# Stick-breaking values with the value block stationary: two heads on 64 output partitions each, split from the bank without transposes

## What is computed

```
h = rmsnorm(x, norm_mix_g);  proj = h @ w_in          # q, k, v of all branches are column ranges of proj
z = einsum('bhqd,bshd->bhqs', q * d**-0.5, k)
log_beta = log_sigmoid(z)
log_1m = where(key < query, log_beta - z, 0)
cum = cumsum(log_1m over keys)
a = where(key < query, exp(log_beta + cum[-1] - cum), 0)
y_sb = einsum('bhqs,bshd->bqhd', a, v)                # [256, 16 * 64]
merged = sig(g_ml)*(y_ml @ w_ml_proj) + sig(g_sc)*(y_sc @ w_sc_proj) + sig(g_sb)*(y_sb @ w_sb_proj)
x = x + merged @ w_out;  x = x + relu(rmsnorm(x) @ w_up)**2 @ w_down;  then the second block
```

## Time and profile before

| | |
|---|---|
| three runs | 957.66, 960.19, 960.67 us; median 960.19 |
| the profiled execution | 958.35 us, of which 956.4 us from first to last instruction; 1.95 us around it |
| TensorE busy | 927.4 us, 97% of the span |
| VectorE, ScalarE, GpSimd busy | 578.9, 469.4, 38.6 us |
| granted TensorE clock, mean | 0.991 of full |
| stick-breaking, from the first scores to the last values | 92.7 to 216.1 us |
| transposes of its result | from 272.8 us |

### The profile page before, as it was taken

One profiled execution on the slowest core, in us unless ns is written; L12 is line 12 of the kernel. 1 busy time (PEld: TensorE's weight loads), 2 busy tenths in 40 slices (PEclk: granted clock), 3 DMA queues, 4 the chain that ended last, 5 costly groups with the idle time before them and its releaser, 6 DMA issues.

```text
span 956.4 us, 14152 instructions
## 1 busy us (share of the span) xinstructions
PE 927.4 (97%) x6003; PEld 841.2 (88%) x6003; DVE 578.9 (61%) x610; ACT 469.4 (49%) x520; POOL 38.6 (4%) x75
## 2 busy tenths in 40 slices
PE   5999999999999999999999999998999799999996
PEld 5998998899998888888999988897888699999885
DVE  4555646577787445556556654556886666666552
ACT  6344776862445434344555534445744554444341
POOL 0000111120010000000000000010000000000000
PEclk9999999999999999999999999998999899999999
DMA  7577444443255556555555565537612465555641
GB/s 266 193 250 229 137 168 139 133 148 117 89 176 177 198 198 195 201 177 198 176 177 177 176 220 181 194 91 247 215 52 87 155 197 178 176 177 198 203 149 44
DMA packets 99374, 164.01 MB, mean 171 GB/s; under 512 B 4832, under 2 KB 37315, under 8 KB 99184
## 3 DMA queue, kind: packets, MB, share of 16 engines
q1 hardware_dynamic: 99312, 163.11, 52.0%
HBM read 162.03 MB, written 3.16 MB: 173 GB/s over the span
## 4 chain that ended last, share of the span: by engine, by line
PE 93%; DVE 2%; DMA 2%; ACT 2%; issue 1%; SPq 1%; POOL 0%; DVEq 0%; ACTq 0%; POOLq 0%
PE acc L509 14%; PE acc L513 14%; PE acc L511 14%; PE acc L501 14%; PE acc L503 14%; PE acc L502 14%; DMA land<-in_w_in 2%; PE m L528 1%; PE m L575 1%; PE m L564 1%; PE m L553 1%; DVE wlo L1211 0%; ACT lw L989 0%; DVE x_tok L1487 0%; PE m L609 0%
## 5 line engine op out<-in xcount | busy, mean ns | idle before, releaser
L1211 DVE TENSOR_TENSOR wlo<-land,whi 128x2048 fp32r<-128x2048 f32 (+2 forms) x153 | 337.1, 2207 | 237.8 <-ACT whi L866 235.2
L866 ACT ACTIVATE whi<-land 128x2048 fp32r<-128x2048 f32 (+2 forms) x153 | 282.3, 1849 | 229.0 <-PE acc L503 156.7
L509 PE MATMUL acc<-xT_hi,whi 128*128 128x256 f32 x1168 | 335.2, 287 | 2.1 <-DVE xT_lo L1248 1.8
L513 PE MATMUL acc<-xT_hi,wlo 128*128 128x256 f32 x1168 | 332.2, 284 | 0.0
L511 PE MATMUL acc<-xT_lo,whi 128*128 128x256 f32 x1168 | 332.1, 284 | 0.0
L509 PEld LDWEIGHTS acc<-xT_hi,whi 128*128 128x128 f32 x1168 | 225.8, 193 | 7.1 <-issue 5.4
L511 PEld LDWEIGHTS acc<-xT_lo,whi 128*128 128x128 f32 x1168 | 225.9, 193 | 0.1
L513 PEld LDWEIGHTS acc<-xT_hi,wlo 128*128 128x128 f32 x1168 | 225.8, 193 | 0.0
L501 PE MATMUL acc<-whi,xT_hi 128*128 128x512 f32 (+2 forms) x240 | 91.4, 381 | 0.0
L503 PE MATMUL acc<-whi,xT_lo 128*128 128x512 f32 (+2 forms) x240 | 90.2, 376 | 0.0
L502 PE MATMUL acc<-wlo,xT_hi 128*128 128x512 f32 (+2 forms) x240 | 90.1, 375 | 0.0
(11 more groups left out here) (337 smaller groups left out, 1074.5 us busy)
## 6 DMA issues: line engine op xcount, KB each, us to landing
land<-in_w_in SPq DMA_DIRECT2D x56, 1024.0 KB, 5.1
land<-in_w_up SPq DMA_DIRECT2D x16, 1024.0 KB, 5.3
land<-in_w_down SPq DMA_DIRECT2D x16, 1024.0 KB, 5.1
land<-in_w_ffn_gate SPq DMA_DIRECT2D x22, 512.0 KB, 4.0
land<-in_w_ffn_up SPq DMA_DIRECT2D x22, 512.0 KB, 5.2
land<-in_w_ffn_down SPq DMA_DIRECT2D x10, 1024.0 KB, 5.1
land<-in_w_out SPq DMA_DIRECT2D x6, 1024.0 KB, 5.0
land<-in_w_in SPq DMA_DIRECT2D x12, 512.0 KB, 4.5
```

Of the source, the lines that this page charges most:

```text
L509: mm(to, whi[:, s, k, cs], xh[:, k0 + k, :], start=first and c % 2 == 0, stop=False, skip_group_check=True)
L513: last = mm(to, wlo[:, s, k, cs], xh[:, k0 + k, :], start=False, stop=end, skip_group_check=True)
L866: activate(whi[:, u % PARTS, 0:m, 0:w], land[:, u % LANDS, 0:m, 0:w], ACT.Copy).then_inc(hi_ready, 1)
L1211: v.tensor_tensor(wlo[:, u % PARTS, 0:m, 0:w], land[:, u % LANDS, 0:m, 0:w], whi[:, u % PARTS, 0:m, 0:w].bitcast(F32), ALU.subtract).then_ ...
```

## The change

The roles in `sb_values` are swapped: the 64 columns of `sbv` that belong to a head are the stationary operand (128 rows by 64 columns), the weights `sba` the moving one. A head's result then has its 64 features on partitions: head h on partitions 0 to 63 and head h+1 on 64 to 127 of the same bank `M[h % 4]`, 256 queries in its first 256 columns. That is the layout the projection takes: tile h // 2 of `ysbT`. `sb_result` becomes a ScalarE copy of 128x256 to `ysbT_hi` and a VectorE subtraction to `ysbT_lo`, once a pair. The stage "ysb" of transposes, with its copies and subtractions, goes. `sb_scores` takes both heads of a pair in one call, the two 256-column matmuls ahead of the two 128-column ones. `sb_av` and `sb_y` count pairs. In the diff the first new `sb_result` is ScalarE's, the second VectorE's.

```
-TURNS = [("x", KD, "norm_mix_g"), ("ysb", KD, None), ("yml", KD, "ml_norm_g"), ("merged", KD, None),
+TURNS = [("x", KD, "norm_mix_g"), ("yml", KD, "ml_norm_g"), ("merged", KD, None),
...
             elif act == "ysbT":
-                turned_ready("ysb", k1)
+                pe.wait_ge(sb_y, k1)
...
         def sb_scores(h):
             if h >= 4:
-                pe.wait_ge(sb_y, h - 3)
+                pe.wait_ge(sb_y, h // 2 - 1)
...
-            c, o = h // 2, SB_D * (h % 2)
-            z = M[h % 4]
-            mm(z[:, 0:T], sbkT[o:o + SB_D, c, 0:P], sbqT[o:o + SB_D, c, :], start=True, stop=True)
-            mm(z[:, T:T + P], sbkT[o:o + SB_D, c, P:T], sbqT[o:o + SB_D, c, P:T], start=False, stop=True,
-               skip_group_check=True).then_inc(sb_z, 1)
+            c = h // 2
+            for i in range(2):
+                hs = slice(SB_D * i, SB_D * (i + 1))
+                mm(M[(h + i) % 4][:, 0:T], sbkT[hs, c, 0:P], sbqT[hs, c, :], start=True, stop=True)
+            for i in range(2):
+                hs = slice(SB_D * i, SB_D * (i + 1))
+                mm(M[(h + i) % 4][:, T:T + P], sbkT[hs, c, P:T], sbqT[hs, c, P:T], start=False, stop=True,
+                   skip_group_check=True).then_inc(sb_z, 1)
...
         def sb_values(h):
-            pe.wait_ge(sb_am, h + 1)
-
-            o, a = M[h % 4][:, 3 * P:], sba[:, h % 2]
-            v = slice(h * SB_D, (h + 1) * SB_D)
-            for to, parts in ((o[:, 0:SB_D], ((0, 0),)), (o[:, SB_D:], ((P, 0), (T, 1)))):
-                for at, t in parts:
-                    last = mm(to, a[:, at:at + P], sbv[:, t, v], start=False, stop=True, skip_group_check=True)
+
+            pe.wait_ge(sb_am, h + 2)
+            to = M[h % 4]
+            for i in range(2):
+                mm(to[SB_D * i:SB_D * (i + 1), 0:T], sbv[:, 0, (h + i) * SB_D:(h + i + 1) * SB_D],
+                   sba[:, i, 0:T], start=True, stop=False, skip_group_check=True)
+            for i in range(2):
+                last = mm(to[SB_D * i:SB_D * (i + 1), P:T], sbv[:, 1, (h + i) * SB_D:(h + i + 1) * SB_D],
+                          sba[:, i, T:3 * P], start=False, stop=True, skip_group_check=True)
             last.then_inc(sb_av, 1)
...
-            if u == TURN_SB:
-                pe.wait_ge(sb_y, SB_H)
-                pe.wait_ge(ml_y, ML_H)
-                turn("ysb", tok)
...
+        def sb_result(h):
+            act.wait_ge(sb_av, h // 2 + 1)
+            activate(ysbT_hi[:, h // 2, :], M[h % 4][:, 0:T], ACT.Copy).then_inc(sb_y_hi, 1)
...
+            if u - SB0 in range(4, SB_H + 3, 2):
+                sb_result(u - SB0 - 4)
             moba_weights((u - 1, UNITS[u - 1][2]))
             if u != LAST_U["mix1"]:
                 split(u + 2)
...
         def sb_result(h):
-            dve.wait_ge(sb_av, h + 1)
-            v.tensor_copy(tok[:, :, h * SB_D:(h + 1) * SB_D],
-                          M[h % 4][:, 3 * P:].rearrange("p (t d) -> p t d", t=TT)).then_inc(sb_y, 1)
+            dve.wait_ge(sb_y_hi, h // 2 + 1)
+            v.tensor_tensor(ysbT_lo[:, h // 2, :], M[h % 4][:, 0:T], ysbT_hi[:, h // 2, :].bitcast(F32),
+                            ALU.subtract).then_inc(sb_y, 1)
```

More of the change, by code:

```diff
@@ L337, in build @@
         sem(n) for n in ("sb_z", "sb_log", "sb_t", "sb_tm", "sb_r", "sb_a", "sb_am", "sb_av", "sb_y"))
-    sig_o = sem("sig_o")
+    sb_y_hi = sem("sb_y_hi")
     ml_s, ml_w, ml_wm, ml_p, ml_num, ml_y, ml_ss, ml_rs, yml_ready = (
@@ L602, in ml_scores @@
                 pe.wait_ge(sb_a, SB_H)
-                pe.wait_ge(sb_y, SB_H)
+                pe.wait_ge(sb_y, SB_H // 2)
                 pe.wait_ge(read_dve, reads_before(G_AT["mlv1"], "dve"))
@@ L819, in _ @@
                     sb_scores(i)
-                    sb_scores(i + 1)
             if i % 2 == 1 and 3 <= i <= SB_H + 1:
                 sb_values(i - 3)
-                sb_values(i - 2)
             i = u - ML0
@@ L920, in sb_weights @@
             if h >= 2:
-                act.wait_ge(sb_av, h - 1)
+                act.wait_ge(sb_av, h // 2)
             activate(sba[:, h % 2], M[h % 4][:, 0:3 * P], ACT.Exp).then_inc(sb_a, 1)
+        def sb_result(h):
+            act.wait_ge(sb_av, h // 2 + 1)
+            activate(ysbT_hi[:, h // 2, :], M[h % 4][:, 0:T], ACT.Copy).then_inc(sb_y_hi, 1)
         def ml_weights(h):
@@ L1121, in _ @@
                 activate(gate[:], acc[:, n % 2], ACT.Sigmoid).then_inc(read_act, 1)
-            if u == TURN_SB:
-                turn_split("ysb", ysbT_hi)
             if u == TURN_ML:
@@ L1530, in _ @@
                 sb_result(u - SB0 - 4)
-                sb_result(u - SB0 - 3)
             if u == B2 + 2:
@@ L1634, in _ @@
             if u == TURN_SB:
-                turn_split("ysb", ysbT_hi, ysbT_lo)
                 dve.wait_ge(ml_rs, 1)
```

## The result

The change takes the median from 960.43 us (four executions, 957.66 to 961.77) to 952.93 us (four, 952.22 to 954.0): a ratio of 0.9919, with a 95% interval of 0.9898 to 0.9940. That is 7.5 us by the medians and 7.8 by the ratio, where the forecast was 4.55 us, or 0.47%. The sign was right and the size was not: the gain is 1.6 to 1.7 times the forecast. The ratio applied to the 960.19 us of the prediction gives 952.4, just under its range; the measured median itself lies just inside.

A forecast was written before the change was run, and what follows sets the result against it. TensorE, busy 97%, was taken as the bound. Transposes 1.75 plus eight values blocks 2.8 made 4.55 us off: 953.8 from the profiled 958.35, 955.6 from the median; forecast 955.0 us, range 952.7 to 957.8.

The forecast's parts named there:

- the clock: Rival: behind TensorE's long second-block waits, a 1.2 GHz stretch comes or goes, about 3 us either way; chance 0.04.
- The sum: TensorE's work: 1.75 us for removed transposes plus 2.8 us for eight values blocks, 4.55 us saved, bounds 4.05 and 4.75.
- The transposes: Near 272.82 us on TensorE: removing them saves 1.67 us plus 0.08 at the next stream matmul, 1.75 us.
- The block: One values block on TensorE, start to next stream matmul: 0.80 us after the change, 0.46 less than now.
- The costs of entering and leaving the tiles: Around each values block: 0.09 us later start, 0.02 us longer first stream matmul behind it.
- The eight blocks: The values blocks of stick-breaking: net 0.35 us saved in each, 2.8 us over eight.
- The two heads side by side: In the values block, two column halves overlap: four 256-column passes take 0.58 us instead of 0.86.
- the serial block: Rival: column halves do not overlap, values block 1.40 us, 1.51 with mode changes, total 959.8 us; chance 0.08.
- Strict order of starts: Rival: matmuls start in program order, 0.215 us more per values block, 1.7 us in all, 956.7 us; chance 0.06.
- The cover of the sums: Before TensorE's sums, 0.3 us left at shorter stream units, no wait; rival that they wait: 962.4 us and more, chance 0.04.
- The order within the scores: In the scores block, issuing both heads' 256-column matmuls ahead of the 128-column ones was costed at nothing.

The follow-up runs named there:

- a_again: The changed kernel run once more, unaltered: 953.72 us, ratio 0.9913 to the kernel before.
- a_fill2: The changed kernel with matmuls nobody reads in front of TensorE's three long waits of the second block: 950.57 us, ratio 0.9888 to the kernel before.
- a_warm: The changed kernel with unread matmuls in the second block's three long waits and 18 more at the very start: 951.82 us, ratio 0.9923 to the kernel before.
- b_short: The kernel before with 36 weight-stream matmuls left out ahead of the second block, 4.3 us less TensorE work: 955.9 us, ratio 0.9937.
- a_turns: The changed kernel with the 16 transposes put back, without the copies and subtractions behind them: 956.39 us, ratio 0.9959 to the kernel before.
- a_one_half: The changed kernel with both heads of a pair on the same column half of the array: 957.01 us, ratio 0.9968 to the kernel before.
- a_copies: The changed kernel with ScalarE's copy of a pair's result made five times, each waiting for the last: 959.7 us, ratio 1.0012 to the kernel before.

## Why the prediction was right or wrong

**The step that failed is the clock.** The prediction priced it (about 3 us either way), gave it 0.04, said that the change "does not alter the waits" and "I have no reason for a side", and let the total follow TensorE's work alone: the term was put at nothing. In the profiled pair the wait at the sigmoids was shorter by 0.38 us, the clock did not fall behind it, which regained 2.96 us, and it fell behind `kl_tok` instead, which cost 1.59. Over all executions, most of them without a trace, the change has the higher mean clocks, worth 1.1 to 1.9 us.

The surplus came twice, 2.9 us by the medians in the result and 3.0 in a_again. Where the waits are filled, most of it is gone: 5.1 and 3.9 us between the kernels by the means (a_fill2, a_warm), with the forecast's 4.55 between them, against 8.1 without fillers on the chip of a_fill2 and 7.1 over all. If the mean clocks, which stayed lower in the filled change, are counted in full, both pairs give 5.6. So the larger part of the surplus is shown to hang on these waits and the clock behind them, and about 1 us is open (0.7 to 1.6 by the executions without fillers at the full count, more at the rate of 0.6). Two things can hold it, and no run held either fixed: the start of the stream at one clock or the other, and the length of the wait at the sigmoids.

Why the clock falls less in the change is not shown either, but the profiles point at that wait. In the seven without fillers it is 2.4 (before), 3.0 (b_short) and 2.8 us (a_turns), and the clock fell behind it each time; in after, a_again, a_one_half and a_copies it is 2.0, 1.6, 1.5 and 1.7, and the clock did not fall. Its length goes with a transfer: ScalarE's last weight split ahead of the sigmoids waits for its block of `in_w_in` for 1.5, 2.4 and 2.2 us in the first three and for 1.4, 1.0, 1.2 and 1.2 in the others. Behind `kl_tok`, after 2.1 us in all seven, the clock fell in after, a_again and a_one_half. What makes that block land earlier in the change is open, and a_turns shows that it need not.

The kernel before had shown part of this. It lost some 4.6 us to 1.2 GHz (2.96 and 1.6, where the prediction had 3.3 and 2.6), as much as the change was meant to give, and both stretches were in the rows. A loss that large, which depends on when waits fall, should have made the range some 3 us wider on the side where it can be regained.

**The sum was right term by term.** The transposes: 1.75 us forecast, 1.75 measured (a_turns). The block: 0.80 forecast from a tile pair in another part of the kernel and half of a scores block, 0.80 measured. The costs of entering and leaving the tiles, 0.09 and 0.02: as read. The eight blocks: 2.8 forecast, 2.78 measured. All of it on TensorE: 4.55 forecast, 4.52 measured. Next to stream matmuls of 512 columns (in front of four blocks and behind four) the gaps are longer in both kernels, 0.23 and 0.32 us in front, 0.32 and 0.34 behind, but the differences are the same 0.09 and 0.02.

**The two heads side by side.** a_one_half gives 1.45 us for the serial block, where the rival had 1.40 (1.51 with the mode changes in front and behind), and the price of losing the overlap, 0.65 a block.

**Strict order of starts.** The block would be 1.0 us; it is 0.80. Strict order would start the four 256-column passes as one, two, one; they start two and two, 0.007 us apart in each pair. The rule that was cited for it, from the Trainium skill ("TensorE: Matmul & The Clock Gate", "Part 3: Packing small matmuls — row/col tiling"), does not hold in this trace for fp32 matmuls of two passes on different tiles.

**The cover of the sums.** Forecast 0.3 us, measured 0.50. ScalarE's copy and VectorE's subtraction at the tight place, then TensorE's request:

```profile
157.85 0.38 ACT L925 ACTIVATE ysbT_hi<-m 128x256 fp32r<-128x256 f32 x1
158.14 1.92 ACT L865 ACTIVATE whi<-land 128x2048 fp32r<-128x2048 f32 x1
```

```profile
159.57 0.41 DVE L1272 TENSOR_TENSOR ysbT_lo<-m,ysbT_hi 128x256 fp32r<-128x256 f32 x1
160.09 2.29 DVE L1214 TENSOR_TENSOR wlo<-land,whi 128x2048 fp32r<-128x2048 f32 x1
162.30 1.02 DVE L1267 TENSOR_TENSOR sbw_lo<-sbw,sbw_hi 128x384 fp32r<-128x384 f32 x2
```

```profile
163.35 0.33 PE L568 MATMUL m<-sbw_hi,sums_r 128*128 128x384 f32 x1
```

The copy took 0.38 us, not up to 0.49, and delayed the split by 0.29 (157.85 to 158.14). The first `sbw_lo` is done at about 162.30 + 0.55 = 162.85, and the sums start at 163.35.

**The order within the scores.** Costed at nothing, and it is nothing: 0.85 us a block (106.81 to 107.66) against 0.86.

```profile
106.81 0.70 PE L555 MATMUL m<-sbqT,sbkT 64*128 64x256 f32 x4
107.34 0.39 PE L558 MATMUL m<-sbqT,sbkT 64*128 64x128 f32 x4
107.66 0.39 PE L509 MATMUL acc<-xT_hi,whi 128*128 128x256 f32 x1
```

## What to carry to other kernels

Where TensorE has no idle time, count its blocks from start to start, and look for the price of a new form in any place of the same kernel that has it: a tile pair in another mixer gave the block to the hundredth. Small matmuls with 64 output columns pay when two of them stand on the two column halves side by side; without the second half, swapping the roles here loses. And before trusting a sum, see what the granted clock costs, by timing a stretch of the program at either clock and not by the mean clock, which also counts time in which TensorE has no work: if the kernel loses about as many microseconds to 1.2 GHz as the change is meant to give, as here, the total can move by much of that, and matmuls without use in the long waits may be worth as much as the change.

## What the hardware showed unexpectedly

- 62 matmuls that nobody needs, put in three waits of 2 to 3.6 us, made both kernels faster: by 5.6 us the kernel before (961.29 to 955.72) and by some 3 us the change (953.72 to 950.57); with 18 more at the start, on another chip, the kernel before gained 3.0 (958.79 to 955.79). They must stand where TensorE really waits: behind another wait they made it late.
- A wait of TensorE of much the same length was followed by a stretch at 1.2 GHz in one execution and not in another: at `kl_tok` after 2.1 us in the change and not after 2.1 us before, where it had fallen at the sigmoids already, and not in a_copies, where it had not.
- Matmuls on a constant during the first transfers brought the full clock early, but in one of two profiles it was lost again before the stream began, at 11.3 us, behind waits of 2.0 and 1.1 us; in the other it stayed through waits of 0.8, 1.1 and 2.5 us.
- A stretch of 6.9 us at 1.2 GHz cost 2.96 us behind the sigmoids, where TensorE is busy for 7.69 of 8 us, and some 1.6 behind `x_tok`, where it is busy for 5.99.
